# Unrooted rows for the router, a reordered VectorE list, and the gate table behind the first transpose

## The reference, cut to what matters

```python
h  = rmsnorm(x, g_ffn)                   # x: 576 rows of 1024, after the mixer's residual
lg = h @ w_router_group  + b_router_group      # 4 logits, argmax -> group
le = h @ w_router_expert + b_router_expert     # 32 logits; top 2 of the chosen group's 8
gates = softmax(lg).max() * top2(softmax(le)) / sum(top2)
for e in range(32):                            # SwiGLU experts, 1024 -> 2*256 -> 1024
    gu  = h @ w_e_in[e]
    out += gates[:, e] * ((silu(gu[:, :256]) * gu[:, 256:]) @ w_e_out[e])
x = x + out
```

## Time and profile before

| | |
|---|---|
| median of 3 executions | 636.81 us (633.6 to 639.97) |
| the profiled execution | 634.51 us, its span 632.6 us |
| TensorE busy | 534.0 us (84%) |
| VectorE / ScalarE / GpSimd busy | 278.9 / 164.4 / 121.7 us |
| DMA | 144.40 MB, mean 228 GB/s |
| mean granted TensorE clock | 0.944 of full |

### The profile page before, as it was taken

How to read it: one execution, slowest core, us unless ns; L and a number is a source line. 1 busy time by engine, 2 the same in 40 slices (tenths; PEclk the granted TensorE clock), 3 DMA queues, 4 the chain that set the end, 5 groups by cost and what they waited for, 6 DMA issues and landing times.

```text
span 632.6 us, 7793 instructions
## 1 busy us (share of the span) xinstructions
PE 534.0 (84%) x2997; PEld 318.1 (50%) x2998; DVE 278.9 (44%) x483; ACT 164.4 (26%) x263; POOL 121.7 (19%) x185
## 2 busy tenths in 40 slices
PE   3999999999989887879999699999987888879600
PEld 2449999998756443334555653434333323323200
DVE  1531899998756644264355742111211111111037
ACT  3222213223767667442111200101010010101112
POOL 3040000321424243100101131211221121100013
PEclk9999999999999998889999689999999798979955
DMA  8702523102305100077732389999999999999575
GB/s 284 201 1 81 187 67 99 37 1 89 118 2 191 76 0 0 1 265 292 297 122 95 134 305 420 421 422 424 423 423 425 425 426 427 427 418 421 225 287 169
DMA packets 42743, 144.40 MB, mean 228 GB/s; under 512 B 6966, under 2 KB 23374, under 8 KB 34007
## 3 DMA queue, kind: packets, MB, share of 16 engines
q1 hardware_dynamic: 38103, 134.78, 54.8%
q0 software_dynamic: 4608, 9.18, 3.8%
HBM read 136.16 MB, written 15.39 MB: 240 GB/s over the span
## 4 chain that ended last, share of the span: by engine, by line
PE 60%; DMA 19%; DVE 7%; SPq 6%; ACT 4%; issue 2%; POOL 1%; DVEq 0%; POOLq 0%; ACTq 0%
PE ps L942 16%; DMA low<-in_w_expert_in 12%; PE ps L1346 9%; PE ps L1167 8%; DMA big<-in_w_expert_out 5%; PE ps L913 4%; PE ps L1371 3%; SPq L605 3%; PE ps L1052 2%; SPq L555 2%; DMA big<-y_dram 2%; PE ps L1049 2%; PE ps L1011 1%; DVE big L1777 1%; PE ps L1030 1%
## 5 line engine op out<-in xcount | busy, mean ns | idle before, releaser
L1711 DVE SCALAR_TENSOR_TENSOR big<-low,cwt,big 128x590 f32<-128x590 f32 x120 | 95.0, 845 | 0.4
L1346 PE MATMUL ps<-big,cw 128*64 128x512 f32 x352 | 83.4, 627 | 10.8 <-issue 5.6
L2067 DVE TENSOR_TENSOR low<-low,ps 128x256 f32<-128x256 f32 x16 | 6.7, 421 | 179.9 <-ACT low L1591 179.9
L942 PE MATMUL ps<-cw_r 128*128 128x288 f32 x256 | 73.0, 295 | 0.0
L942 PE MATMUL ps<-low_r,cw_r 128*128 128x288 f32 x256 | 72.9, 294 | 0.0
L942 PE MATMUL ps<-cw_r,big_r 128*128 128x288 f32 x256 | 72.7, 294 | 0.0
L1167 PE MATMUL ps<-cw,low 128*128 128x512 f32 x128 | 58.2, 608 | 3.8 <-DVE low L1821 3.8
L1346 PEld LDWEIGHTS ps<-big,cw 128*64 128x64 f32 x352 | 30.0, 144 | 62.4 <-issue 62.4
L942 PEld LDWEIGHTS ps<-cw_r 128*128 128x128 f32 x256 | 47.4, 188 | 0.4 <-issue 0.4
L942 PEld LDWEIGHTS ps<-cw_r,big_r 128*128 128x128 f32 x256 | 47.2, 188 | 0.0
L942 PEld LDWEIGHTS ps<-low_r,cw_r 128*128 128x128 f32 x256 | 47.2, 187 | 0.0
(11 more groups left out here) (260 smaller groups left out, 770.7 us busy)
## 6 DMA issues: line engine op xcount, KB each, us to landing
big<-in_w_expert_in SPq DMA_DIRECT2D x20, 2048.0 KB, 24.0
big<-in_w_expert_out SPq DMA_DIRECT2D x22, 1024.0 KB, 26.7
low<-in_w_expert_in SPq DMA_DIRECT2D x8, 2048.0 KB, 24.4
big<-in_w_in SPq DMA_DIRECT2D x20, 512.0 KB, 4.7
low<-in_w_expert_out SPq DMA_DIRECT2D x10, 1024.0 KB, 31.5
cw<-in_w_out SPq DMA_DIRECT2D x1, 4096.0 KB, 14.0
low<-in_w_expert_in SPq DMA_DIRECT2D x4, 1024.0 KB, 34.5
big<-in_w_expert_in SPq DMA_DIRECT2D x4, 1024.0 KB, 27.8
```

Source lines behind the costliest of these rows:

```text
L942: return pe.matmul(ps[:, proj_bank(j) + half, 0:HALF], w[:, k, :], h[:, k, cols], start=first, stop=last, skip_group_check=True)
L1346: mm = pe.matmul(ps[TILE * half:TILE * half + TILE, GU_BANK[s], :], xt[s][:, k, TILE * half:TILE * half + TILE], wi[2 * s + half][:, k, :] ...
L1711: ins = dve.scalar_tensor_tensor(conv[:, i, :], u[:, i, j:j + CW], cwt[:, i, j:j + 1], conv[:, i, :], ALU.mult, ALU.add)
```

## The change

`normed_h2` is cut in two. `gain_h2(c)` multiplies by `g_ffn`, makes the variance and counts the new semaphore `gained`. `normed_h2(c)` is left with the multiplication by the root, in place, and so waits until TensorE has transposed the rows (`h2_turned`). `turn_h2(c)` waits for `gained` in place of `h2_ready`; the DMA to `h2_dram` still waits for `h2_ready`. The logits now come from rows without the root, and the first instruction of `choose(c)` multiplies them by it as it adds the bias. VectorE's list is reordered: `choose(2)` between the two parts of chunk 3, and `place_at(2)` ahead of `normed_h2(4)` and `choose(3)`. TensorE's `gate_table` moves behind `turn(0)`, and VectorE's `copy_xt(0, 0)` ahead of `gates_in`. The lists of ScalarE, GpSimd and SyncE are as they were.

```diff
@@ -310,6 +310,7 @@
         x2_ready = sem("x2_ready")
         ssq2_ready = sem("ssq2_ready")
         h2_ready = sem("h2_ready")
+        gained = sem("gained")
         h2_turned = sem("h2_turned")
         h2t_ready = sem("h2t_ready")
         logit_done = sem("logit_done")
@@ -1211,7 +1212,7 @@
             turn_co()
             def turn_h2(c):
                 w = ROWS[c]
-                pe.wait_ge(h2_ready, c + 1)
+                pe.wait_ge(gained, c + 1)
                 if c >= 1:
                     pe.wait_ge(h2t_ready, c)
                 else:
@@ -1320,7 +1321,6 @@
             table(3)
             table(4)
             busy(WARM)
-            gate_table()
 
             def turn(g, s, n):
                 pe.wait_ge(gathered[s], n * 16 + 16)
@@ -1384,6 +1384,7 @@
 
 
             turn(0, 0, 0)
+            gate_table()
             pair_loop(pe, step, tail=4)
 
             def more(n, e, t):
@@ -1892,7 +1893,7 @@
                         cols = slice(512 * n, 512 * n + 512)
                         dve.tensor_tensor(x[0:w, c, cols], x[0:w, c, cols], ps[w * n:w * n + w, 4 + n, :], ALU.add).then_inc(x2_ready, 1)
 
-            def normed_h2(c):
+            def gain_h2(c):
 
                 w = ROWS[c]
                 h = h2[c % 2][0:w, :]
@@ -1915,7 +1916,14 @@
                     dve.wait_ge(ssq2_ready, c + 2)
                     dve.scalar_tensor_tensor(stat[0:w, 32 + c:33 + c], stat[0:w, 45:46], 1.0 / D, stat[0:w, 8 + c:9 + c],
                                              ALU.mult, ALU.add).then_inc(var_ready, 1)
-                link(times_gain(slice(KD // 2, KD)))
+                times_gain(slice(KD // 2, KD)).then_inc(gained, 1)
+
+            def normed_h2(c):
+
+                w = ROWS[c]
+                h = h2[c % 2][0:w, :]
+                dve.wait_ge(gained, c + 1)
+                dve.wait_ge(h2_turned, c + 1)
                 rooted[0] += 1
                 dve.wait_ge(rstd_ready, rooted[0])
                 dve.tensor_scalar(h, h, stat[0:w, 32 + c:33 + c], None, ALU.mult).then_inc(h2_ready, 1)
@@ -1925,7 +1933,7 @@
                 w = ROWS[c]
                 lgg, lge = lg[0:w, c, 0:NG], lg[0:w, c, NG:NG + NE]
                 dve.wait_ge(logit_done, c + 1)
-                link(dve.tensor_tensor(lg[0:w, c, :], ps[0:w, 2 + c % 2, 0:36], bias36[0:w, :], ALU.add))
+                link(dve.scalar_tensor_tensor(lg[0:w, c, :], ps[0:w, 2 + c % 2, 0:36], stat[0:w, 32 + c:33 + c], bias36[0:w, :], ALU.mult, ALU.add))
                 link(dve.tensor_reduce(gmax[0:w, c:c + 1], lgg, AX.X, ALU.max))
                 link(dve.scalar_tensor_tensor(gscore[0:w], lgg, gmax[0:w, c:c + 1], fall4[0:w], ALU.is_equal, ALU.mult))
                 link(dve.tensor_reduce(gfirst[0:w], gscore[0:w], AX.X, ALU.max))
@@ -1975,22 +1983,27 @@
             link(dve.scalar_tensor_tensor(beyond, colid, float(S0), beyond, ALU.is_lt, ALU.mult))
             link(dve.tensor_scalar(low2.rearrange("p c k f -> p c (k f)"), wide(colid, 4), -BIGF, None, ALU.add))
             link(dve.tensor_scalar(low2[:, :, 1, 1], low2[:, :, 1, 1], float(COLS), None, ALU.add))
+            gain_h2(0)
+            residual(1)
             normed_h2(0)
-            residual(1)
+            gain_h2(1)
             normed_h2(1)
             residual(2)
-            normed_h2(2)
+            gain_h2(2)
             choose(0)
             choose(1)
             place_at(0)
+            normed_h2(2)
             residual(3)
             place_at(1)
+            gain_h2(3)
+            choose(2)
             normed_h2(3)
-            choose(2)
             residual(4)
+            gain_h2(4)
+            place_at(2)
             normed_h2(4)
             choose(3)
-            place_at(2)
             for c in range(2):
                 places(c)
                 entries(c)
@@ -2078,8 +2091,8 @@
                 if not (peeled(g) and g == PAIRS - 1):
                     copy_xt(g + 1, (s + 1) % RING)
 
+            copy_xt(0, 0)
             gates_in()
-            copy_xt(0, 0)
             further_tiles()
             pair_loop(dve, step, tail=1)
 
```

## The result

The changed kernel takes 643.72 us in the median of 4 executions (641.13 to 645.13), the kernel before 635.66 us (633.6 to 639.97): ratio 1.0105, 95% interval 1.0063 to 1.0146. A second comparison with 12 executions of the changed kernel and 29 of the kernel before gave 641.48 against 637.5 us, ratio 1.0062 (1.0036 to 1.0089). So it is slower by 0.6 to 1%, some 4 to 7 us. The profiled execution took 643.28 us, its span is 641.4 us: 8.8 us more than before.

What follows compares the result with a forecast made beforehand. The prediction took the experts' stage as bound by its weight loads, the end following gathered[0]. Later router +1.1 and clock +0.9 gave +2.0 us: 636.8 + 2.0 = 638.8 us, range 634 to 643.

Steps and rivals of the forecast that it cites:

- the broken stream: Rival: gate_up(0) at half clock frees the first slot 5 to 7 us later; +4 to +6 us, 641 to 643; chance 0.08.
- What bounds the kernel: Experts' stage: bound by the transfer of weights; the end follows gathered[0] and its load, not the first expert matmul.
- The added wait: VectorE: normed_h2(3) waits for turn_h2(3), so residual(4) behind it starts at 347.9, 1.6 us later, delaying logits(3).
- The product of `normed_h2(3)`: VectorE, ahead of residual(4): multiplication of chunk 3 by the root, 1024 columns, entered at 0.75 us.
- late for nobody: Root of chunk 4, with the 2.66 us buffer clearing in front, done at about 352.3 and delaying no engine.
- The clock's term: TensorE's clock may fall in the longer pause ahead of logits(3): 0 to 2.3 us, taken as 0.9.
- the order: Part of the forecast from the cut normed_h2 and new VectorE order: everything behind choose(4) comes 1.1 us later.
- Part 2: gate_table behind turn(0): TensorE gains 1.4 us, worth nothing at the end; output-weight load 3.1 us behind the other, covered.
- TensorE decides: Rival: the end follows gate_up(0) and residual(4) isn't held up; -1.7 us, 635.1 us; chance 0.12.
- The wait doesn't bite: Rival: VectorE's list hides the wait for turn_h2(3), but the stream decides; -0.3 us, 636.5; chance 0.08.
- More than I see: Rival: the change helps in the first 346 us, where TensorE would be late now; -3 us, 634; chance 0.05.

Runs made afterwards that it cites:

- gate_only: Kernel before with only the gate table's move (TensorE's gate_table behind turn(0), VectorE's copy_xt(0, 0) ahead of gates_in): 637.09 against 637.5 us, ratio 1.0001.
- early_load: Kernel before without SyncE's wait for the first gather ahead of the load of pair 2's second input weights: 635.71 against 636.37 us, ratio 0.9986.
- clear_on_scalar: Changed kernel with the clearing of the gather buffers moved from GpSimd to ScalarE behind copy_h2t(4): 641.3 against 636.37 us for the kernel before, ratio 1.0049.
- best: Changed kernel, residual(4) and gain_h2(4) ahead of normed_h2(3), choose(3) ahead of normed_h2(4), clearing on ScalarE, no SyncE gather wait: 642.97 us, ratio 1.0097 to before.
- residual_first: Changed kernel with residual(4) ahead of normed_h2(3) in VectorE's list: 638.19 against 637.5 us for the kernel before, ratio 1.0003.
- repaired: The kernel of `best` with SyncE's wait for the first gather put back: 634.9 against 635.55 us for the kernel before, ratio 0.999.
- repaired_sooner: `repaired` with SyncE's load waiting for idx_ready 2 (gather issued) instead of the gather's landing: 634.66 against 635.55 us for the kernel before, ratio 0.9984.

## Why the prediction was right or wrong

**The size.** The forecast was +2.0 us with bounds of +0.8 and +3.6. The load behind the gather moved by 5.0 us in both traces, the last load by 4.6 to 4.7, and the longer comparison of times gives +4.0 us, with 2.3 to 5.7 as its interval. So the sum came out at half of what was measured or less, and in the traces outside its own bounds. The range of 634 to 643 us holds the median of the longer comparison (641.48) and not that of the first (643.72); that it reached so far up is owed to a rival that didn't happen, the broken stream, and to the spread of the runs. That is luck.

**What bounds the kernel: right, with a condition.** The load behind the gather moved by +5.0 us, and the stream behind it moved along; TensorE's 1.5 us from the gate table came to nothing (`gate_only`). `early_load` shows the condition: the load is the start of the stream only while the two that follow it are in time.

**The added wait: right in place and in its chain.** `normed_h2(3)` held `residual(4)`, that held ScalarE's squares and copy, and these `logits(3)`; `choose(3)` behind the wait of `normed_h2(4)`, `choose(4)` behind both. The swap of two calls removes 4.2 us.

**Two terms were mis-sized, and they make up 2.6 of the 3.0 us between 2.0 and 5.0.** The product of `normed_h2(3)` was entered at 0.75 us; it took 2.16. I had GpSimd's clearing in the same sum (346.32 to 348.98) and counted it only as a delay of the root: "late for nobody". That it stood beside a VectorE product for the first time, I didn't ask: +1.4 us. A row of before could have misled me further. The multiplication of two SBUF tensors in chunk 4's `times_gain`, first half, ran beside the clearing and took its usual time:

```profile
347.83 1.10 DVE L1905 TENSOR_TENSOR low<-x,low 64x512 f32<-64x512 f32 x1
```

So the clearing doesn't slow every instruction of VectorE. The Trainium skill, "GPSIMD Engine Reference", "Specifications", says that GpSimd and VectorE share their SBUF interfaces, and that VectorE instructions in a two-port mode or with two SBUF inputs contend. The Trainium skill, "VectorE: DVE Perf Modes", "Mode 2×_2P — use both read ports for one tensor", counts a product with a scalar among those that can use that mode. The product is indeed the faster kind here (1024 elements a row in 0.75 us, the multiplication of two tensors 512 in 1.1). The traces agree for the product (2.16 against 0.75 us), and disagree for the multiplication of two tensors (1.10 us beside the clearing, 1.06 to 1.10 elsewhere). That holds for this neighbour, which only writes, and for an instruction on 64 rows; no run has another pair. The two pages would have warned of the collision, though not of its length, had I asked them of the new neighbour.

The clock's term stood between 0 and 2.3 us, and I took 0.9. It was 2.1, near the upper bound, in both traces. The two terms hang together: in `clear_on_scalar`, with 2.45 us of pause, near my 2.3, the clock fell only in `logits(3)`, and `logits(3)` and `turn_h2(4)` together lost 1.3 us. In the changed kernel the product stretched the pause to 3.85 us, and the clock fell inside it. The sum by these terms is 1.1 (the order, taken from the forecast, for no run has it alone) + 1.4 + 2.1 = 4.6. Some 0.4 us remain: `logits(3)` started 0.1 and the product on chunk 4 another 0.2 later than these terms say. I take these for steps between engines that I had rounded down; no run shows it.

**Part 2 was right**: the gate table's load came 2.9 us behind the other instead of 2.1, and it was covered.

**The rivals.** "TensorE decides" is out: `gate_only` gave TensorE 1.5 us, and the last load of weights stayed within 0.2 us of its place. "The wait doesn't bite" is out. "The stream breaks" didn't happen in this kernel, but its mechanism is real: `best` shows `gate_up(0)` at half clock for part of its time, and the queue low behind it (115 GB/s in 384 to 386 us). "More than I see" in the first 346 us shows no sign: the place of the fillers is spread alike with both lists. For a chance of slower by over 1% I had said 0.09; the first comparison lies just above that mark and the longer one below it.

## What to carry to other kernels

Where an in-order list gets a new wait, look at the next instruction behind it: here a store-side product that nobody needed soon stood ahead of the residual that everybody waited for, and moving it one place down was worth 4.2 us. When a step moves in time, list what the other engines do at its new place, not only who waits for whom. And a program bound by a stream has a start that may consist of several loads; to move one of them ahead of a gather, look at what the others wait for, and let the gather go out first.

## What the runs showed of the hardware

- A VectorE product of 128x1024 by a per-row scalar takes 0.75 us, but beside a GpSimd clearing of 128x3072 (2.66 us) it ends only 0.5 to 0.6 us after that does; a multiplication of two SBUF tensors (1.10 us) ran beside the same clearing unhindered.
- TensorE's clock stayed full over a pause of 0.7 us ahead of `logits(3)` and through `logits(3)` in every trace that has one; in pauses of 3.85 us it fell to half (1.2 GHz), 3.1 us into one and 2.1 us into the other, and sixteen records of 128x36 took 3.60 us instead of 1.95. A short pause was no safeguard for what came next: in `residual_first`, `repaired`, `repaired_sooner` and `early_load`, with pauses of at most 0.72 us since the fillers, the clock fell 4.6 to 4.8 us behind the fillers' start, in or next to `turn_h2(4)`.
- A gather of 0.5 MB that was issued 1.6 us behind a load of 2 MB (`best`) brought its rows 6.9 us after its issue, some 3.3 us later than the 3.5 to 3.7 of the other runs in which the load waits for it; a load issued when the gather had just been issued (363.96 against 362.32 to 363.60 us) didn't hold it up: `turn(0)` began 3.5 us after the gather's issue without a wait, and `gate_up(0)` 21.5 us behind the fillers' start, with 21.7 in `repaired`.
- In a stage bound by the load of weights, the last load followed the load that opened the stream by 196.1 to 196.5 us in ten traces, whatever TensorE did: `gate_up(0)` stood 2.5 to 4.3 us behind that load.
